# Six of eight gate tiles moved from the projection into the chunk loop of a local attention layer, and gating moved to the head of the output product

## The reference

```python
proj = h @ w_in                          # q 1024, k 256, v 256, g 1024 columns
q, k = partial_rope(q), partial_rope(k)  # 16 query heads, 4 key heads of 64
s = jnp.einsum('bcqhgd,bckhd->bhgcqk', qc, kb) * (SW_HEAD ** -0.5)
m = jnp.maximum(jnp.max(s, axis=-1, keepdims=True), sink)
p = jnp.exp(s - m)
p = p / (jnp.sum(p, axis=-1, keepdims=True) + jnp.exp(sink - m))
o = jnp.einsum('bhgcqk,bckhd->bcqhgd', p, vb).reshape(B, T, SW_WIDTH)
o = o * jax.nn.silu(g.astype(F32))
return o.astype(h.dtype) @ w_out
```

## Time and profile before

| what | value |
|---|---|
| device time, median of 3 runs | 1651.21 us (1645.47 to 1654.92) |
| profiled execution: its time, its span | 1651.35 us, 1649.6 us |
| PE busy, instructions | 1452.7 us, 88%, 8443 |
| DVE busy | 764.0 us, 46% |
| ACT busy | 415.9 us, 25% |
| POOL busy | 73.0 us, 4% |
| granted clock of PE, mean | 0.946 |
| gate tiles in `sw_project` | 619.09 to 674.24 us of the span |
| `sw_attend` | 680.07 to 720.26 us of the span |

### The profile page before, as it was taken

One profiled execution on the slowest core, in us unless ns is written; L12 is line 12 of the kernel. 1 busy time (PEld: TensorE's weight loads), 2 busy tenths in 40 slices (PEclk: granted clock), 3 DMA queues, 4 the chain that ended last, 5 costly groups with the idle time before them and its releaser, 6 DMA issues. The chain is left out here.

```text
span 1649.6 us, 20443 instructions
## 1 busy us (share of the span) xinstructions
PE 1452.7 (88%) x8443; PEld 778.0 (47%) x8443; DVE 764.0 (46%) x1695; ACT 415.9 (25%) x890; POOL 73.0 (4%) x54
## 2 busy tenths in 40 slices
PE   5989999676998999899899998598989999765998
PEld 2434544565634444654544345444434544565633
DVE  5894571557353001432243102706894481558352
ACT  1130420555401011531012302101130420554401
POOL 0000410210000000000000000000000310110000
PEclk9999999897999999999799899799999999897999
DMA  6212121101500222102122121023212221101401
GB/s 198 64 51 77 51 75 40 52 2 53 208 0 0 64 77 76 40 27 77 27 77 76 51 64 38 1 64 121 64 39 76 64 64 51 53 2 53 157 13 51
DMA packets 108772, 100.63 MB, mean 61 GB/s; under 512 B 4156, under 2 KB 98660, under 8 KB 107656
## 3 DMA queue, kind: packets, MB, share of 16 engines
q1 hardware_dynamic: 108104, 97.23, 19.0%
q10 hardware_dynamic: 576, 2.10, 0.3%
HBM read 88.83 MB, written 10.49 MB: 60 GB/s over the span
## 5 line engine op out<-in xcount | busy, mean ns | idle before, releaser
L887 PE MATMUL bank<-arena 128*128 128x512 f32 x1024 | 450.9, 599 | 9.5 <-DVE arena L640 7.5
L887 PEld LDWEIGHTS bank<-arena 128*128 128x128 f32 x1024 | 195.0, 192 | 257.2 <-issue 241.3
L845 PE MATMUL bank<-arena 64*64 64x64 f32 (+3 forms) x4672 | 197.6, 245 | 62.2 <-DVE arena L751 23.6
L845 PEld LDWEIGHTS bank<-arena 64*64 64x64 f32 (+2 forms) x4672 | 175.0, 152 | 92.3 <-issue 53.1
L298 PE MATMUL bank<-arena 128*128 128x512 f32 x256 | 112.0, 600 | 10.7 <-PEq L1984 9.6
L1222 PE MATMUL bank<-arena 128*128 128x512 f32 x256 | 117.0, 612 | 3.0 <-DVE arena L1182 3.0
L1672 PE MATMUL bank<-arena 128*128 128x512 f32 x256 | 111.5, 597 | 0.0
L512 ACT ACTIVATE arena<-bank 128x512 f32<-128x512 f32 x48 | 28.7, 597 | 275.7 <-PE bank L887 275.5
L159 ACT ACTIVATE arena<-arena 128x1024 f32<-128x1024 f32 x20 | 21.1, 1055 | 271.2 <-DVE arena L1190 142.5
L298 PEld LDWEIGHTS bank<-arena 128*128 128x128 f32 x256 | 49.1, 193 | 72.2 <-issue 72.2
L1222 PEld LDWEIGHTS bank<-arena 128*128 128x128 f32 x256 | 48.7, 195 | 70.4 <-issue 64.8
(11 more groups left out here) (220 smaller groups left out, 1598.6 us busy)
## 6 DMA issues: line engine op xcount, KB each, us to landing
arena<-in_rw_w_in SPq DMA_DIRECT2D x66, 512.0 KB, 4.0
arena<-in_ml_w_in SPq DMA_DIRECT2D x24, 512.0 KB, 3.9
arena<-in_sw_w_in SPq DMA_DIRECT2D x20, 512.0 KB, 3.7
spill<-arena SPq DMA_DIRECT2D x4, 2048.0 KB, 8.3
arena<-spill SPq DMA_DIRECT2D x4, 2048.0 KB, 8.2
arena<-in_rw_w_out SPq DMA_DIRECT2D x16, 512.0 KB, 7.3
arena<-in_sw_w_out SPq DMA_DIRECT2D x8, 512.0 KB, 3.3
arena<-in_ml_w_out SPq DMA_DIRECT2D x8, 512.0 KB, 3.2
```

The lines of the kernel that those rows point to most:

```text
L845: mm = lambda out, a, b, start=True, stop=True: nc.tensor.matmul(out, a, b, start=start, stop=stop, skip_group_check=True)
L887: last = nc.tensor.matmul(bank[:, :], slot[:, k, :], mix_at[what][:, k, :], start=k == 0, stop=k == KT - 1)
```

## The change

Two gate tiles stay in `sw_project` (`SW_EARLY_G`). The other six, their weights, products, sigmoids and multiplications, go into `sw_attend`, one in each round of the chunk loop, with two banks of their own (6 and 7). The banks come from the scores, which now have one set of two banks instead of two: scores run one chunk ahead, and scores(c) waits until the exponentials of chunk c - 1 have been taken. `gate(dve, c)` becomes `keep(dve, c)`, a copy of the output to Y, and Y is multiplied by G in `stage_out`, in eight pieces of 512 columns, with PE waiting for piece k ahead of its row k.

```diff
@@ stage_out
-def stage_out(m, y_at, n0, norm):
+def stage_out(m, y_at, n0, norm, gate_at=None):
...
                 m.weights_arrived(pe, n0 + k)
+                if gate_at is not None:
+                    pe.wait_ge(gated.handle, gated.at(k + 1))
...
             norm.clear(dve)
+            if gate_at is not None:
+                G = m.view(gate_at, KT, T)
+                for k in range(KT):
+                    nc.vector.tensor_tensor(Y[:, k, :], Y[:, k, :], G[:, k, :], ALU.mult).then_inc(gated.handle, 1)
@@ sw_project
-            m.load_weights(sp, n0 + 20 + SLOTS)
+            m.load_weights(sp, n0 + 12 + SW_EARLY_G + SLOTS)
...
-            for j in range(KT):
+            for j in range(SW_EARLY_G):
                 m.weights_arrived(pe, w)
                 slot = m.view(m.slot(w), KT, P)
-                if j < 4:
-                    pe.wait_ge(qkv_evac.handle, qkv_evac.at(4 + j + 1))
-                else:
-                    pe.wait_ge(g_used.handle, g_used.at(j - 3))
+                pe.wait_ge(qkv_evac.handle, qkv_evac.at(4 + j + 1))
@@ sw_attend
+            m.load_weights(sp, n0 + len(g_tiles) + SLOTS)
...
-        def gate(dve, c):
+        def keep(dve, c):
             dve.wait_ge(o_done.handle, o_done.at(c + 1))
-            nc.vector.tensor_tensor(Y[:, :, c * C:(c + 1) * C], m.bank[6 + c % 2][:, :].rearrange("p (k t) -> p k t", t=C),
-                                    G[:, :, c * C:(c + 1) * C], ALU.mult).then_inc(o_evac.handle, 1)
+            nc.vector.tensor_copy(Y[:, :, c * C:(c + 1) * C], m.bank[4 + c % 2][:, :].rearrange("p (k t) -> p k t", t=C))\
+                .then_inc(o_evac.handle, 1)
...
             def scores(c):
-                if c >= 2:
-
-                    pe.wait_ge(s_exp.handle, s_exp.at(c - 1))
+                if c >= 1:
+
+                    pe.wait_ge(s_exp.handle, s_exp.at(c))
                 for h in range(8):
-                    bank = m.bank[2 * (c % 2) + h // 4]
+                    bank = m.bank[h // 4]
...
+            def gate_products(i):
+                m.weights_arrived(pe, n0 + i)
+                if i >= 2:
+                    pe.wait_ge(g_used.handle, g_used.at(i - 1))
+                for k in range(KT):
+                    last = nc.tensor.matmul(g_bank(i)[:, :], m.view(m.slot(n0 + i), KT, P)[:, k, :], xt[:, k, 1:T + 1],
+                                            start=k == 0, stop=k == KT - 1)
+                last.then_inc(g_done.handle, 1)
+
             scores(0)
-            scores(1)
+            gate_products(0)
             for c in range(NC):
-                if c + 2 < NC:
-                    scores(c + 2)
+                if c + 1 < NC:
+                    scores(c + 1)
                 turn(c)
                 if c >= 1:
                     outputs(c - 1)
+                if c + 1 < len(g_tiles):
+                    gate_products(c + 1)
             outputs(NC - 1)
...
+            def sigmoid(i):
+                act.wait_ge(g_done.handle, g_done.at(i + 1))
+                nc.scalar.activation(G[:, g_tiles[i], :], g_bank(i)[:, :], ACT.Sigmoid).then_inc(g_sig.handle, 1)
 
             exps(0)
             for c in range(NC):
                 if c + 1 < NC:
                     exps(c + 1)
                 evac(act, c)
+                if c < len(g_tiles):
+                    sigmoid(c)
...
+            def gate(i):
+                dve.wait_ge(g_sig.handle, g_sig.at(i + 1))
+                nc.vector.tensor_tensor(G[:, g_tiles[i], :], g_bank(i)[:, :], G[:, g_tiles[i], :], ALU.mult)\
+                    .then_inc(g_used.handle, 1)
...
                 if c >= 2:
-                    gate(dve, c - 2)
-            gate(dve, NC - 2)
-            gate(dve, NC - 1)
+                    keep(dve, c - 2)
+                if 1 <= c <= len(g_tiles):
+                    gate(c - 1)
+            keep(dve, NC - 2)
+            keep(dve, NC - 1)
@@ encoder
-                sw_attend(m)
-                stage_out(m, S_Y, b, next_norm(n + 1, pairs_of_banks, B_R))
+                sw_attend(m, a + 12 + SW_EARLY_G)
+                stage_out(m, S_Y, b, next_norm(n + 1, pairs_of_banks, B_R), S_G)
```

More of the change, by code:

```diff
@@ L284, in stage_out @@
     m.used_by += [(rows_used.handle, rows_used.at(k + 1)) for k in range(KT - 1)] + [(done.handle, done.at(8))]
-    added = m.sem("h_added")
+    added, gated = m.sem("h_added"), m.sem("g_gated")
     with nc.Block() as block:
@@ L324, in stage_out @@
     norm.finish()
+    gated.base += 0 if gate_at is None else KT
     done.base += 8
@@ L1283 @@
 SW_KV = 4
+SW_EARLY_G = 2
 def sw_project(m, sinks, n0):
@@ L1301, in sw_project @@
     m.used_by += [(rows_used.handle, rows_used.at(7 + k + 1)) for k in range(3)] + [(q_done.handle, q_done.at(12))]
-    m.used_by += [(g_done.handle, g_done.at(k + 1)) for k in range(KT)]
+    m.used_by += [(g_done.handle, g_done.at(k + 1)) for k in range(SW_EARLY_G)]
     count = [0]
@@ L1407, in _, with sw_attend @@
                 nc.vector.tensor_copy(vs[64:128, i, :], qkv[0:64, i + 1, 1280:1536])
-            for j in range(KT):
+            for j in range(SW_EARLY_G):
                 dve.wait_ge(sig_done.handle, sig_done.at(j + 1))
                 nc.vector.tensor_tensor(G[:, j, :], m.bank[4 + j % 4][:, :], G[:, j, :], ALU.mult).then_inc(g_used.handle, 1)
-    for s, n in ((rows_used, 10), (q_done, 12), (qkv_evac, 12), (g_done, KT), (sig_done, KT), (g_used, KT), (turned, 10),
+    for s, n in ((rows_used, 10), (q_done, 12), (qkv_evac, 12), (g_done, SW_EARLY_G), (sig_done, SW_EARLY_G), (g_used, SW_EARLY_G), (turned, 10),
                  (turn_evac, 10), (chain, count[0]), (sink, 32), (rotated, NT)):
         s.base += n
-def sw_attend(m):
+def sw_attend(m, n0):
     nc = m.nc
@@ L1432, in sw_attend @@
         "o_evac", "dve_chain", "sinks_loaded"))
+    g_done, g_sig, g_used = (m.sem(n) for n in ("tile_done", "act_evacuated", "g_gated"))
+    xt = m.view(A_XT, KT, T + 1)
+    g_tiles = list(range(SW_EARLY_G, KT))
+    g_bank = lambda i: m.bank[6 + i % 2]
+    m.used_by += [(g_done.handle, g_done.at(i + 1)) for i in range(len(g_tiles))]
     count = [0]
@@ L1446, in evac @@
                     act.wait_ge(o_done.handle, o_done.at(c - 1))
-                nc.scalar.activation(pt[c % 2][0:keys(c), 4 * q:4 * q + 4, :], m.bank[4 + q][0:keys(c), :], ACT.Copy)\
+                nc.scalar.activation(pt[c % 2][0:keys(c), 4 * q:4 * q + 4, :], m.bank[2 + q][0:keys(c), :], ACT.Copy)\
                     .then_inc(p_evac.handle, 1)
@@ L1470, in turn @@
                     for k in range(4):
-                        last = nc.tensor.transpose(m.bank[4 + q][0:keys(c), P * k:P * k + P], prob[c % 2][:, 4 * q + k, 0:keys(c)],
+                        last = nc.tensor.transpose(m.bank[2 + q][0:keys(c), P * k:P * k + P], prob[c % 2][:, 4 * q + k, 0:keys(c)],
                                                    ident)
@@ L1484, in outputs @@
                         at = C * (h // 2 + 4 * f)
-                        last = nc.tensor.matmul(m.bank[6 + c % 2][out, at:at + C], v[0:keys(c), C * kv:C * kv + C],
+                        last = nc.tensor.matmul(m.bank[4 + c % 2][out, at:at + C], v[0:keys(c), C * kv:C * kv + C],
                                                 pt[c % 2][0:keys(c), h, C * f:C * f + C], start=True, stop=True,
@@ L1532, in maxima @@
                 for q in range(2):
-                    bank = m.bank[2 * (c % 2) + q][:, :].rearrange("p (h k) -> p h k", k=P)[:, :, 0:keys(c)]
+                    bank = m.bank[q][:, :].rearrange("p (h k) -> p h k", k=P)[:, :, 0:keys(c)]
                     ins = nc.vector.tensor_reduce(st[:, 0, 4 * q:4 * q + 4], bank, AX.X, ALU.max)
```

4 lines of the change are left out of this document (3 added, 1 removed).

## The result

The changed kernel takes 1691.6 us (median; 1688.07 to 1694.75), the kernel before 1651.25 us beside it: a ratio of 1.0236, 95% interval 1.0212 to 1.0261. It is slower by 40.4 us. The forecast was 1677 us with a range of 1668 to 1688: the sign and the mechanism hold, the size does not. Ratios are of executions at the kernels' usual granted clock; one execution of one experiment, 1833.8 us at a mean clock of 0.82, is left out.

What follows compares the result with a forecast made beforehand. PE, busy 88% of the span, was taken to set the time, with ACT and DVE near its pace in attention. Net +19.6 us for rounds less tiles, +0.8 head, +6 clock: 1651.3 to 1677.7, taken as 1677 us, range 1668 to 1688.

Steps and rivals of the forecast that it cites:

- Removed tiles: In the projection, six gate tiles of 6.89 us each leave PE, which ran them without a pause: -41.36 us.
- The wait behind the single set of banks: In `sw_attend`, PE's transposes wait behind scores(c + 1) for maxima and normalisation: 3.82 us in each round, where none was.
- The rounds laid end to end: Attention rounds of 14.76 us with a tile, 7.87 without: stage +60.94 us, against 41.36 removed, leaving +19.6 us.
- Table loads, head, transfers: 12 more ACT table loads (15.4 us) cost nothing, gating at the output's head +0.8 us, ten weight transfers nothing.
- The granted clock: In attention, the new waits bring PE clock falls, 0 to 1.65 us each, 0 to 11.6 in all; taken as +6 us.
- A low clock that stays: Rival: each clock fall in attention lasts through half a tile more, 12 us on top of all falls: 1696 us; chance 0.10.
- Gaps filled: Rival: tiles run where PE would wait in attention, the stage shrinks by its 7.16 us gap: 1643 us; chance 0.05.
- break-even of 0.9 us of wait per round: For the gaps-filled rival in attention: below 0.9 us of PE wait per round the change gains; 3.82 was forecast.
- ACT as the bound: Rival: in attention, ACT's table loads stand behind the waits and delay chunk 7's exponentials: 1680 to 1683 us; chance 0.08.
- The wait absorbed: Rival: weights, engines and barriers hide most of the 27 us of waits, for a net of nothing; chance 0.05.

## Why the prediction was wrong, point by point

**Removed tiles: right.** Two tiles take 13.91 us, so 6.9 us each, and six are gone from the projection.

**The wait behind the single set of banks: right.** 3.77 us was measured for 3.82, six times, and 3.24 in the first round, whose chunk has half the keys; from scores to transposes it was 5.74 us for 5.72. The run with one set of banks and no tile shows that the banks alone bring it, and the run with the normalisation first shows that it hangs on DVE's order.

**The rounds laid end to end: right.** 19.6 us, with 0.8 for the head, against 21.3 us for the layer with the waits filled. The 0.9 us over is mostly rounds with a tile of 14.95 us (661.91 to 676.86 there) in place of 14.76: a tile with the way into it takes some 7.07 us, not 6.89.

**Table loads, head, transfers: right.** 12 more ACT instructions, none on the path; 0.87 us at the head for 0.8.

**The granted clock: the step that failed.** The prediction said "each fall adds between 0 and 1.65 us: 0 to 11.6 us" and "I take +6 us". Measured: 16.2 us, 2.3 us a fall. The mechanism was right (every one of the seven waits, longer than the one that had brought a fall, brought one); the size came from a single fall of some 3.3 us, where the seven falls of the changed kernel lasted 44.4 us together, 6.3 each. In the kernel before, the clock fell just as PE went back to work (0.76 in the window of 685 to 686 puts it at 685.52, the scores at 685.56). Behind waits of 3.77 us it mostly falls while PE still waits, and then it stays low for 6.8 us. Of that 0.3 to 1.7 us lie in the wait and cost nothing; the rest runs at half speed. So the upper bound of the term was no bound: it priced the number of falls, and took the length of one for granted. That is 10.2 of the 14.6 us between 1677 and 1691.6. Another 0.9 us is the rounds, 0.7 us is the rounding of the sum to 1677, and the remaining 2.8 us lie outside the layer, in code that is the same; what moved them isn't known.

The page TensorE: Matmul & The Clock Gate of the Trainium skill, section A second HAM failure mode, says of another kernel that frequent short idle pauses of PE between groups of products make the clock go back and forth between its two levels. The seven falls agree; it gives no length for the low stretch behind a wait of this kind, which this trace puts at 6.8 us in six of seven.

**The rivals.** "A low clock that stays", with half a tile more for each fall and 1696 us, had the length nearly right and got 0.10: six of seven falls lasted 3.4 us longer than the one seen, which is half a tile. Its price, 23.6 us with all falls, was too high, because part of each fall lay in the wait; 16.2 was measured. And the argument against it, the tiles, did not keep a fall at 3.4 us: all four of the falls of 6.8 us that had a tile behind their wait ended only inside it. Gaps filled: only once all eight tiles were in and DVE's order was another. Its break-even of 0.9 us of wait per round is not contradicted: 3.77 us lost 40 us, none gained 2.9 us in the layer. ACT as the bound: out, by the run without switches. The wait absorbed: out, the seven waits stand in the trace with 25.9 us and the layer is 37.5 us longer.

## What to carry to other kernels

When a buffer is given up to make room, look at every in-order engine for a step that stood ahead of another only because its input was always there: with less look-ahead that order becomes a wait, and swapping two steps can be worth most of the loss. Independent work must stand where the engine would wait, in every round, the last ones too; work that merely sits in the same loop fills nothing. And a wait of PE is to be priced with the fall that it may bring: here 3.77 us of wait cost about 6 us. No one length parted waits with a fall from those without: in these runs 1.85 us brought one and 2.63 us did not.

## What the runs showed of the hardware that was not expected

In this layer's attention the length of a low stretch went with when the clock fell: 3.4 us in all eleven falls that came with PE at work, 6.8 us or more in all twenty-two with more than 0.4 us of the wait ahead. A wait needn't be filled whole to avoid most of this: with 1.7 us of products in a wait of 3.8 us, two waits of seven brought a fall, and 3.4 us each. And in the kernel with eight tiles, whose rounds run transposes and the small products of scores and outputs for 4 us out of 11, the clock stayed at 1.00 for the whole stage of 89.82 us.
